# The mixer's output projection in two groups of 1024 columns, with seven block products in four of its units

## The chip, the cores and the metric

One core of one Trainium2 chip runs the kernel as a single program. The time is device microseconds of one execution; the median of three runs stands for a kernel. Engines have names of two kinds here: TensorE is PE in the profile, VectorE is DVE, ScalarE is ACT, GpSimd is POOL and SyncE is SP.

## The reference, cut to what matters

The model is two blocks on 256 tokens of width 2048, in float32. The change lies in the first block, where the token mixer ends and its norm and the cross attention begin:

```python
    merged = jax.nn.sigmoid(m_a) * (y_a @ w_proj_a) + jax.nn.sigmoid(m_b) * (y_b @ w_proj_b)
    return merged @ w_out                       # [256, 2048] @ [2048, 2048]
...
    x = x + rmsnorm(y, post_norm_mix[l])        # y is what the mixer returned
    h = rmsnorm(x, pre_norm_xa[l])
    m = rmsnorm(mem, mem_norm_g[l])
    y = memory_cross_attention(h, m, xa_wq[l], xa_wk[l], xa_wv[l], xa_wo[l])
```

rmsnorm divides a token's row by the root of the mean of its squares and multiplies it by a gain per column.

## The kernel before, in words

**Precision.** Every operand x is kept as a high part (fp32r, a rounded copy) and a low part (x minus the high part). A product is three matmuls: high by high, low operand by high weight, high operand by low weight. Weights are split while the kernel runs. SyncE loads a unit of weights (1 MiB) into one of three buffers `raw`. ScalarE copies it into `wh` (`split_hi`), VectorE writes raw minus wh into `wl` (`split_lo`), and a raw buffer is loaded again once its low part is made.

**Groups and units.** All large products are groups in one list (`groups_of`), in the order in which they run. A group is a range of output columns and is cut into units along the contraction. The kinds are: "feat" (256 columns, result turned, units of 8 k-blocks of 128), "tok" (512 columns, tokens on partitions, units of 4 k-blocks) and "wide" (1024 columns, units of 2 k-blocks). Units of the last two kinds have 24 matmuls of 512 columns. Results lie in four PSUM banks: two sets of two (`ps`). A feat or tok group uses one set, and the groups alternate. A wide group uses all four: token half 0 in the set of the group before, token half 1 in its own. Its first unit starts with token half 1 and waits for the other two banks before token half 0. Its last unit ends with token half 1. Four more banks (`pm`) serve small work.

**The stretch of the change.** The groups run mb0 to mb7 (gate), pb0 to pb7 (w_proj_b; the evacuation `evac_pb` makes the merged operand mg, 256 features a group), wo0 to wo3 (w_out, tok), xk0, xk1 (keys of the cross attention), xq0, xq1 and so on. wo's evacuation: ScalarE squares each 512-column bank for the norm's sums, then VectorE multiplies the bank by the norm's gain (`gb`) into yA. `norm1a` and `norm1b` make x1 and its scaled copy in yA, TensorE turns yA in `h2_a` (before xk1's last unit) and `h2_b` (before xq0), and both other engines split what was turned.

**Seven products.** The FFN's down projection (dw00, dw01, dw10) is wide, and in four units of each (`SEVEN`) it makes a two-by-two block product from seven products instead of eight: 21 matmuls. It needs four combinations of the operand's blocks (the forms, made once and split) and four differences of the weight's blocks (`dif_lo` and `dif_hi`, per unit: VectorE three instructions, ScalarE two, VectorE two). Some of the products gather in `pm` banks; `dw_sums` adds these into the output tile, and `evac_dw` adds the ps banks to it.

**Order of the work.** Each engine has its own strict program, written by a loop over the units. `BESIDE` maps (group, slot) to small stages that run beside a unit. For unit n, VectorE runs in this order: the stages of slot n, the differences of unit n+1 if that has seven products, token half 0 of a wide group's evacuation if n is its last unit, the low part of unit n+2, the stages of the half slot, and only then the evacuation of the group if n was its last. ScalarE runs: the high differences, the high part of unit n+2, the stages, the evacuation. Three stages of the memory's norm lie here: `mem_scale` (roots, at pb6), `mem_spread` (a small product on TensorE) and `mem_split` in four parts (sixteen instructions on each of ScalarE and VectorE). POOL loads `mem_in` (2 MiB) when mem_scale is done, `gb` after pb7, and the token rows `xx` after the last mem_split.

Of the kernel before, what the change touches and what calls it, by code (L numbers as in the profile page):

```python
# [5 lines left out]
F = mybir.dt.float32  # L6
R = mybir.dt.float32r
# [105 lines left out]
def groups_of(I):  # L113
# [28 lines left out]
    for i in range(4):  # L142
        add("wo%d" % i, I["w_out"][0], KC, [(512 * i, 512)], "tok", "mg")
# [7 lines left out]
    for half in range(2):  # L151
# [7 lines left out]
        for i in range(2 - half):  # L159
            add("dw%d%d" % (half, i), down, HF, [(1024 * i, 1024)], "wide", "ac", chunk=2, k_off=half * HF)  # L160
# [19 lines left out]
def units_of(groups):  # L180
# [63 lines left out]
    "dw00_sums": 4, "dw01_sums": 4, "dw10_sums": 4,  # L244
# [27 lines left out]
SEVEN = (2, 4, 6, 8)  # L272

# [4 lines left out]
def build(nc, I, cst_d, out_d):  # L278
# [13 lines left out]
    def by_part(both):  # L292
# [87 lines left out]
    junk_wo = tile("junk_wo", B + 4, [128, 512])  # L380
# [23 lines left out]
    dif, dif_l = [[[tile("%s%d%d" % (name, half, q), (XT if half else B) + 4 * q, [128, 1024], dt) for q in range(2)]  # L404
                   for half in range(2)] for name, dt in (("dif", F), ("dif_l", R))]
    dif_h = [[tile("dif_h%d%d" % (half, q), kb, [128, 1024], R) for q, kb in enumerate(at)]
             for half, at in enumerate(((C + 16, M + 12), (XT + 8, XT + 12)))]
# [41 lines left out]
    bst = tile("bst", B, [128, 2, 48])  # L449

# [131 lines left out]

    seven = [u.n for u in units if u.g.kind == "wide" and u.ui in SEVEN]

# [135 lines left out]
    def tensor_program(p):  # L720
# [421 lines left out]

        def wide(u):

            h, l = parts(u.n)
            p.wait_ge(*hi_ready(u.n))
            half = int(u.g.k_off > 0)
            p.wait_ge(*ready("ac", u.k + 1, half, 0))
            if u.last:
                wide_products(u, (0,), h, (ach, acl), "")  # L1150
                p.wait_ge(*lo_ready(u.n))
                wide_products(u, (0,), l, (ach,), "last").then_inc(s_acc, 1)
                wide_products(u, (1,), h, (ach, acl), "").then_inc(s_high, 1)
                wide_products(u, (1,), l, (ach,), "last").then_inc(s_used, 1)
                return
            if u.ui == 0:
                for tb in (1, 0):
# [4 lines left out]
                    t = wide_products(u, (tb,), h, (ach, acl), "")  # L1162
            else:
                t = wide_products(u, (0, 1), h, (ach, acl), "")
            t.then_inc(s_high, 1)
            p.wait_ge(*lo_ready(u.n))
            wide_products(u, (0, 1), l, (ach,), "").then_inc(s_used, 1)

        def seven_products(u):

            h, l = parts(u.n)
            half, m, j = int(u.g.k_off > 0), seven.index(u.n), 4 * SEVEN.index(u.ui)
            k, new, end = u.k, u.ui == SEVEN[0], u.ui == SEVEN[-1]
# [4 lines left out]
            a11, a12, a22 = [[x_[:, kk, t_] for x_ in (ach, acl)] for kk, t_ in ((k, lo_t), (k + 1, lo_t), (k + 1, hi_t))]  # L1178
            s1, s2, s3, s4 = [[f[:, j + i, :] for f in (form_h, form_l)] for i in range(4)]
            q11, q21, q22 = slice(0, 512), slice(1024, 1536), slice(1536, 2048)  # L1180
            p.wait_ge(*hi_ready(u.n))
            p.wait_ge(*ready("ac", k + 1, half, 0))
# [10 lines left out]
            for q, pairs in enumerate((((p5, s1, sums[1]), (p7, s3, sums[2])), ((p6, s2, sums[3]), (b21, a22, None)))):  # L1193
                d, dh = dif_l[half][q], dif_h[half][q]
# [98 lines left out]
    def scalar_program(a):  # L1293
# [37 lines left out]
        def dif_hi(n):  # L1331

            half, m = int(units[n].g.k_off > 0), seven.index(n)
            if m:
                a.wait_ge(s_diffree, m)
            for q in range(2):
                a.wait_ge(s_dif, 2 * m + q + 1)
                act(dif_h[half][q], dif[half][q], ACT.Copy).then_inc(s_difh, 1)

        def dw_sums(name):  # L1340
# [3 lines left out]
            if name == "dw10":  # L1344
# [149 lines left out]
        def evac_wo(i, blocks):  # L1494
            name = "wo%d" % i
            for tb in blocks:
                filled(name, tb)
                j = tb * 4 + i
                square("junk_wo", junk_wo, ps[set_of[name]][tb], cell("part1", 8)[:, j:j + 1])

        def norm1a():
            root("p1", 2)
            a.wait_ge(s_a2v, last["junk_wo"])
# [10 lines left out]
        def h2(part, k0):  # L1514
            a.wait_ge(s_used, after("wo3"))
# [240 lines left out]
        def evac_w2(i, blocks):  # L1756
# [11 lines left out]
            "gla_turn4": lambda: gla_turn(4), "gla_turn8": lambda: gla_turn(8), "gla_turn12": lambda: gla_turn(12),  # L1768
            "mem_sums": mem_sums, "mem_scale": mem_scale, "mem_split0": lambda: mem_split(0),
# [19 lines left out]
        def evac(name, blocks):  # L1789
# [17 lines left out]
            elif kind == "wo":  # L1807
                evac_wo(i, blocks)
# [70 lines left out]
    def vector_program(v):  # L1879
# [69 lines left out]
        def dif_lo(n):  # L1949

            half, m, r = int(units[n].g.k_off > 0), seven.index(n), v3(raw[n % 3], 512)
            d = [v3(dif[half][q], 512) for q in range(2)]
            v.wait_ge(s_ac, 11 * half + 11)
# [8 lines left out]
            for q in range(2):  # L1962
                v.wait_ge(s_difh, 2 * m + q + 1)
                lo_part(dif_l[half][q], dif[half][q], dif_h[half][q]).then_inc(s_difl, 1)
# [276 lines left out]
        def evac_pb(i):  # L2241
# [14 lines left out]
            lo_part(xtl[:, c, :], v3(m_, 256), xth[:, c, :]).then_inc(s_mg, 1)  # L2256

# [25 lines left out]
        def evac_wo(i, blocks):  # L2283
            name = "wo%d" % i
            c = slice(512 * i, 512 * i + 512)
            v.wait_ge(s_gb1, 16)
            v.wait_ge(s_used, after("pb7"))
            for tb in blocks:
                filled(name, tb)
                heard()  # L2290
                tt(yA[:, tb, c], ps[set_of[name]][tb], gb[:, c], ALU.mult).then_inc(s_accfree[set_of[name]], 1)

        def norm1a():
            v.wait_ge(*evacuated("wo2"))
            v.wait_ge(*evacuated("wo3"))
            ssq = cell("ssq1", 2)
            t = own.add(v.tensor_reduce(ssq, v3(cell("part1", 8), 4), AX.X, ALU.add))
# [20 lines left out]
        def h2(part, k0):  # L2318
            v.wait_ge(s_used, after("wo3"))
# [198 lines left out]
        def dw_sums(name):  # L2518
# [504 lines left out]
        def layer_norm(tb, scaled):  # L3023
# [37 lines left out]
            "gla_turn4": lambda: gla_turn(4), "gla_turn8": lambda: gla_turn(8), "gla_turn12": lambda: gla_turn(12),  # L3061
            "mem_sums": mem_sums, "mem_scale": mem_scale, "mem_spread": mem_spread, "mem_split0": lambda: mem_split(0),
# [28 lines left out]

        def evac(name, blocks):
            kind, i = name[:-1], int(name[-1]) if name[-1].isdigit() else 0
            if kind == "u":
# [22 lines left out]
            elif kind == "wo":  # L3117
# [235 lines left out]
```

## Time and profile before

| what | value |
|---|---|
| median of 3 runs | 2054.79 us (2054.45 to 2055.03) |
| span of the profiled execution, first to last instruction | 2053.1 us |
| TensorE busy | 2044.2 us |
| VectorE busy | 1524.8 us |
| ScalarE busy | 988.5 us |
| mean granted clock of TensorE | 1.000 |
| weights and data read | 392.09 MB, 193 GB/s over the span |

The span is what the trace shows of the profiled execution; the device time of the runs lies 1.7 us above it at the median. Busy time is the time in which an engine has an instruction in work. An idle time in a timeline stands behind the instruction that follows it, with the engine and tile that ended it. Tiles that share a place in memory share names in the profile: a unit's tiles are raw, wh and wl, the merged operand and the turned ones are xt.

### The profile page before, as it was taken

Reading aid. Unit: us, or ns where it says so; the run is one execution under the profiler, and the core shown is the slowest. Engines: PE = TensorE matmul, PEld = TensorE weight load, DVE = VectorE, ACT = ScalarE, POOL = GpSimd, SP = SyncE. Lnnn points to the kernel's source line nnn. Section 1 sums busy time; section 2 is a strip of 40 time slices with the busy share of each in tenths; the row PEclk is TensorE's granted clock in tenths of the full one; section 3 lists DMA queues with packets and bytes.
Section 4 is the critical chain, followed back from the end, with each engine's and each line's share of the span. In section 5 each row is a group of like instructions: output and inputs, shape, how many; then the busy total and the mean of one; then the engine's idle time right before and its main releaser. Section 6 shows DMA issues by size and latency. Waiting matters only on the chain.

```text
span 2053.1 us, 26543 instructions
## 1 busy us (share of the span) xinstructions
PE 2044.2 (100%) x10788; PEld 1757.5 (86%) x10788; DVE 1524.8 (74%) x1857; ACT 988.5 (48%) x986; POOL 16.0 (1%) x34
## 2 busy tenths in 40 slices
PE   9999999999999999999999999999999999999999
PEld 7888888888888888888888888888888888888987
DVE  5776786554656767678988887888886768987776
ACT  6443363454444455555554544445454434454642
POOL 0000000000000000000000000000000000000000
PEclk9999999999999999999999999999999999999999
DMA  9766656546566765555656565555566654554462
GB/s 328 220 191 194 193 167 213 180 153 210 152 198 226 259 233 185 184 186 174 209 191 200 189 202 188 194 189 192 198 212 236 185 174 144 186 184 144 144 244 105
DMA packets 298346, 397.99 MB, mean 194 GB/s; under 512 B 18945, under 2 KB 223793, under 8 KB 296561
## 3 DMA queue, kind: packets, MB, share of 16 engines
q1 hardware_dynamic: 294096, 375.28, 56.1%
q0 software_dynamic: 3408, 18.92, 2.5%
q10 hardware_dynamic: 720, 2.11, 0.3%
q8 instruction: 85, 1.39, 0.3%
q14 instruction: 37, 0.30, 0.0%
HBM read 392.09 MB, written 4.19 MB: 193 GB/s over the span
## 4 chain that ended last, share of the span: by engine, by line
PE 97%; DVE 1%; DMA 1%; ACT 1%; issue 0%; SPq 0%; DVEq 0%; ACTq 0%
PE ps L723 91%; PE pm L723 5%; PE pm L726 1%; DVE wl L1884 0%; DMA raw<-in_w_in 0%; DMA xin<-in_x_by_features 0%; DVE cv L1892 0%; ACT wh L1298 0%; ACT xt L1298 0%; DVE yA L1884 0%; DVE up L2066 0%; ACT cv L1298 0%; DVE up L1884 0%; ACT L1298 0%; DVE xt L1892 0%
## 5 line engine op out<-in xcount | busy, mean ns | idle before, releaser
L1884 DVE TENSOR_TENSOR wl<-raw,wh 128x2048 fp32r<-128x2048 f32 (+2 forms) x368 | 790.0, 2161 | 284.0 <-ACT wh L1298 211.6
L1298 ACT ACTIVATE wh<-raw 128x2048 fp32r<-128x2048 f32 (+1 forms) x357 | 664.1, 1873 | 318.6 <-PE ps L723 268.4
L723 PE MATMUL ps<-xt,wh 128*128 128x512 f32 (+2 forms) x2736 | 638.4, 389 | 0.2 <-ACT wh L1298 0.2
L723 PEld LDWEIGHTS ps<-xt,wh 128*128 128x128 f32 (+1 forms) x2736 | 505.0, 188 | 101.7 <-issue 0.7
L723 PE MATMUL ps<-wh,xt 128*128 128x512 f32 x1600 | 387.1, 391 | 1.8 <-ACT wh L1298 1.8
L723 PEld LDWEIGHTS ps<-wh,xt 128*128 128x128 f32 x1600 | 298.1, 188 | 64.5 <-issue 1.6
L723 PEld LDWEIGHTS ps<-xt,wl 128*128 128x128 f32 x2704 | 336.3, 192 | 7.0
L723 PE MATMUL ps<-xt,wl 128*128 128x256 f32 x2704 | 338.6, 283 | 0.0
L723 PE MATMUL ps<-wl,xt 128*128 128x512 f32 x800 | 203.0, 390 | 0.4 <-DVE wl L1884 0.4
L723 PEld LDWEIGHTS ps<-wl,xt 128*128 128x128 f32 x800 | 149.9, 188 | 32.7 <-DVE wl L1884 1.7
L1298 ACT ACTIVATE cv<-up,vt 128x256 f32<-128x256 f32 x88 | 52.5, 601 | 220.3 <-DVE up L1884 220.3
L723 PE MATMUL ps<-wh,ach 128*128 128x512 f32 x268 | 104.6, 390 | 0.4 <-DVE yA L1884 0.4
L723 PE MATMUL ps<-wh,acl 128*128 128x512 f32 x268 | 104.3, 389 | 0.0
L1892 DVE SCALAR_TENSOR_TENSOR cv<-up,vt,cv 128x255 f32<-128x255 f32 (+1 forms) x176 | 81.0, 481 | 6.6 <-ACT cv L1298 3.5
L723 PE MATMUL ps<-wl,ach 128*128 128x512 f32 x268 | 69.2, 389 | 0.0
L723 PEld LDWEIGHTS ps<-wh,ach 128*128 128x128 f32 x268 | 50.3, 188 | 11.8 <-DVE yA L1884 0.8
L723 PE MATMUL ps<-ybT,wh 128*128 128x512 f32 x256 | 59.9, 390 | 0.0
L723 PEld LDWEIGHTS ps<-wl,ach 128*128 128x128 f32 x268 | 50.3, 188 | 10.5
L723 PEld LDWEIGHTS ps<-wh,acl 128*128 128x128 f32 x268 | 50.3, 188 | 10.3
L2066 DVE TENSOR_REDUCE up<-ps 128x256 f32<-128x512 f32 x84 | 57.2, 684 | 0.0
L723 PEld LDWEIGHTS ps<-ybT,wh 128*128 128x128 f32 x256 | 47.4, 188 | 9.4
L1298 ACT ACTIVATE dif_h<-dif 128x1024 fp32r<-128x1024 f32 x24 | 25.5, 1063 | 50.4 <-DVE dif L1884 50.4
(405 smaller groups left out, 1601.5 us busy)
## 6 DMA issues: line engine op xcount, KB each, us to landing
raw<-in_w_in SPq DMA_DIRECT2D x146, 1024.0 KB, 5.3
raw<-in_ffn_w_up SPq DMA_DIRECT2D x84, 1024.0 KB, 5.2
raw<-in_ffn_w_down SPq DMA_DIRECT2D x43, 1024.0 KB, 5.1
raw<-in_w_out SPq DMA_DIRECT2D x32, 1024.0 KB, 5.3
raw<-in_w_proj_b SPq DMA_DIRECT2D x16, 1024.0 KB, 5.4
raw<-in_w_proj_a SPq DMA_DIRECT2D x8, 1024.0 KB, 5.4
raw<-in_xa_wk SPq DMA_DIRECT2D x4, 1024.0 KB, 5.4
raw<-in_xa_wq SPq DMA_DIRECT2D x4, 1024.0 KB, 5.3
```

The source lines that it names most:

```text
L723: return p.matmul(out, l, r, start=start, stop=stop, skip_group_check=share)
L726: return p.transpose(out, a, ident)
L1298: return a.activation(out, in_, func, bias=bias, scale=scale)
L1884: return v.tensor_tensor(out, a, b, op)
L1892: return v.scalar_tensor_tensor(out=out, in0=a, scalar=s, in1=b, op0=op0, op1=op1)
L2066: v.tensor_reduce(out, halves, AX.X, ALU.add).then_inc(s_accfree[set_of[name]], 1)
```

## The change

wo becomes two wide groups of eight units. Units 2 and 5 of each have seven products. The forms of the merged operand are made in the evacuations of pb2 and pb5 and lie in SBUF below the former lowest tile, in room that the software DMA queue's scratch gives up (16 KB to 4 KB). The stages at wo move to new slots. The evacuation now adds banks and sums into yA, ScalarE squares yA from SBUF (two instructions of 1024 columns a group), and VectorE multiplies by the gain in an instruction of its own behind that (`s_gain`). The wait on the operand in wide units stays only in the first group that uses it.

```diff
+SCRATCH = 4096
+LOW = (SCRATCH + 128 - BASE) // KB
...
-    for i in range(4):
-        add("wo%d" % i, I["w_out"][0], KC, [(512 * i, 512)], "tok", "mg")
+    for i in range(2):
+        add("wo%d" % i, I["w_out"][0], KC, [(1024 * i, 1024)], "wide", "mg", chunk=2, seven=PAIRS["mg"])
...
-    ("pb4", 0): ["mem_sums"], ("pb6", 0): ["mem_scale"], ("wo0", 2): ["mem_spread"],
-    ("wo1", 0): ["mem_split0"], ("wo1", 1): ["mem_split4"], ("wo1", 2): ["mem_split8"], ("wo1", 3): ["mem_split12"],
+    ("pb4", 0): ["mem_sums"], ("pb6", 0): ["mem_scale"], ("wo0", 0): ["mem_spread"],
+    ("wo0", 2.5): ["mem_split0"], ("wo0", 3): ["mem_split4"], ("wo0", 5.5): ["mem_split8"], ("wo0", 6): ["wo0_sums", "mem_split12"],
+    ("wo1", 6): ["wo1_sums"],
...
+PAIRS = {"mg": (2, 5), "ac": SEVEN}
...
 # ScalarE, evac_pb
             to_v.add(act(xth[:, 2 * i:2 * i + 2, :], v3(mt[i % 2], 256), ACT.Copy))
+            if i in PAIRS["mg"]:
+                j = PAIRS["mg"].index(i)
+                heard()
+                to_v.add(act(mg_form_h[:, 4 * j:4 * j + 4, :], v3(mg_form[j], 128), ACT.Copy))
...
 # ScalarE, evac_wo
-                filled(name, tb)
-                j = tb * 4 + i
-                square("junk_wo", junk_wo, ps[set_of[name]][tb], cell("part1", 8)[:, j:j + 1])
+                for n in range(2):
+                    a.wait_ge(*evacuated("wo%d" % i, 2 * tb + n))
+                j = tb * 2 + i
+                square("junk_m", junk_m, yA[:, tb, 1024 * i:1024 * i + 1024], cell("part1", 4)[:, j:j + 1])
...
 # VectorE, evac_pb: behind the low part of xt, if i in PAIRS["mg"]
+            tt(s1, a21, a22, ALU.add)
+            step(own.add(tt(s3, a21, a11, ALU.subtract)))
+            step(own.add(tt(s2, s3, a22, ALU.add)))
+            to_act.add(tt(s4, a12, s2, ALU.subtract))
+            heard()
+            lo_part(mg_form_l[:, 4 * j:4 * j + 4, :], v3(mg_form[j], 128), mg_form_h[:, 4 * j:4 * j + 4, :]).then_inc(
+                s_form["mg"], 1)
...
 # VectorE, evac_wo
-                heard()
-                tt(yA[:, tb, c], ps[set_of[name]][tb], gb[:, c], ALU.mult).then_inc(s_accfree[set_of[name]], 1)
+            i = int(name[2])
+            step(last[name])
+            filled(name, tb)
+            for n in range(2):
+                o = yA[:, tb, 1024 * i + 512 * n:1024 * i + 512 * n + 512]
+                tt(o, bank(name, 2 * tb + n), o, ALU.add).then_inc(evacuated(name, 2 * tb + n)[0], 1)
+            if tb:
+                c = slice(1024 * i, 1024 * i + 1024)
+                v.wait_ge(s_gb1, 16)
+                for b in range(2):
+                    heard()
+                    tt(yA[:, b, c], yA[:, b, c], gb[:, c], ALU.mult).then_inc(s_gain, 1)
...
 # VectorE, norm1a
-            v.wait_ge(*evacuated("wo2"))
-            v.wait_ge(*evacuated("wo3"))
+            v.wait_ge(s_gain, 4)
```

## Rows read from the trace of the kernel before

**Rows 1.** The page, part 1: busy us, share of span, instructions.
```profile
PE 2044.2 (100%) x10788; PEld 1757.5 (86%) x10788; DVE 1524.8 (74%) x1857; ACT 988.5 (48%) x986; POOL 16.0 (1%) x34
```

**Rows 2.** Windows: busy us (x count) by engine, granted clock, DMA share, GB/s.
```profile
680.00:830.00 150.00, 150.00 (x764) 128.27 (x763) 104.04 (x113) 78.70 (x93) 4.19 (x8) 1.00 0.69 238
```

**Rows 3.** TensorE timeline in wo2: start, duration us, what [idle before <-releaser].
```profile
742.42 3.79 PE L723 MATMUL ps<-wh,xt 128*128 128x512 f32 x16
...
747.86 3.79 PE L723 MATMUL ps<-wh,xt 128*128 128x512 f32 x16
```

**Rows 4.** Timeline, VectorE: the FFN's equivalent of the forms.
```profile
966.50 0.49 DVE L1884 TENSOR_TENSOR up<-cv 128x128 f32<-128x128 f32 x2
...
968.87 0.69 DVE L1884 TENSOR_TENSOR form_l<-up,form_h 128x512 fp32r<-128x512 f32 x1 [1.22 <-ACT form_h L1298]
```

**Rows 5.** Timeline of ScalarE, pb2 to pb7.
```profile
646.85 3.71 ACT L1298 ACTIVATE wh<-raw 128x2048 fp32r<-128x2048 f32 x2
...
683.71 1.28 ACT L1298 ACT_TABLE_LOAD   x1
...
686.12 1.90 ACT L1298 ACTIVATE wh<-raw 128x2048 fp32r<-128x2048 f32 x1
...
697.82 1.92 ACT L1298 ACTIVATE wh<-raw 128x2048 fp32r<-128x2048 f32 x1 [1.42 <-DMA raw<-in_w_out]
```

**Rows 6.** Timeline of VectorE, pb3 to pb7.
```profile
652.31 2.29 DVE L1884 TENSOR_TENSOR wl<-raw,wh 128x2048 fp32r<-128x2048 f32 x1 [1.23 <-PE ps L723]
...
678.35 1.28 DVE L2066 TENSOR_REDUCE mt<-ps 128x256 f32<-128x512 f32 x2
...
686.65 4.49 DVE L1884 TENSOR_TENSOR wl<-raw,wh 128x2048 fp32r<-128x2048 f32 x2
...
701.98 1.28 DVE L2066 TENSOR_REDUCE mt<-ps 128x256 f32<-128x512 f32 x2
...
705.55 0.69 DVE L1884 TENSOR_TENSOR xt<-mt,xt 128x512 fp32r<-128x512 f32 x1 [0.70 <-ACT xt L1298]
```

**Rows 7.** Timeline of TensorE: pb7 begins, wo0 begins.
```profile
687.30 7.44 PE L723 MATMUL ps<-ybT,wh 128*128 128x512 f32 x32
...
698.41 3.82 PE L723 MATMUL ps<-wh,xt 128*128 128x512 f32 x16
```

**Rows 8.** Timeline of VectorE in wo1: the low parts of memT.
```profile
727.64 1.67 DVE L1892 SCALAR_TENSOR_TENSOR memT<-mem_in,vt,memT 128x256 fp32r<-128x256 f32 x4
```

**Rows 9.** VectorE timeline where dw00 ends and dw01 begins.
```profile
1194.17 1.28 DVE L1884 TENSOR_TENSOR yA<-ps,yA 128x512 f32<-128x512 f32 x2
...
1195.37 1.82 DVE L1884 TENSOR_TENSOR wl<-raw,wh 128x512 fp32r<-128x512 f32 x2
...
1197.10 1.22 DVE L1884 TENSOR_TENSOR dif<-raw 128x1024 f32<-128x1024 f32 x1
```

**Rows 10.** Timeline of TensorE at the same place.
```profile
1195.60 0.47 PE L723 MATMUL ps<-wh,ach 128*128 128x512 f32 x1 [0.41 <-DVE yA L1884]
```

**Rows 11.** Timeline of VectorE behind the projection.
```profile
787.73 0.17 DVE L2297 TENSOR_REDUCE st<-st 128x2 f32<-128x8 f32 x1
...
799.35 1.29 DVE L1888 TENSOR_SCALAR yA<-xx,st 128x2048 f32<-128x2048 f32 x1
...
806.88 3.22 DVE L1892 SCALAR_TENSOR_TENSOR xt<-pm,vt,xt 128x256 fp32r<-128x256 f32 x8
```

**Rows 12.** TensorE timeline: xk0 begins, then the turns of yA.
```profile
785.94 3.79 PE L723 MATMUL ps<-memT,wh 128*128 128x512 f32 x16
...
802.63 1.91 PE L726 MATMUL pm<-cst,yA 128*128 128x128 f32 x16
...
809.97 1.91 PE L726 MATMUL pm<-cst,yA 128*128 128x128 f32 x16
```

**Rows 13.** By tile junk_m: count, ns min/median/max, first and last start.
```profile
L1318 ACT ACTIVATE junk_m<-xx x4: 1042/1058/1063, 659.8 to 663.4; 128x1024 f32<-128x1024 f32 x4
```

**Rows 14.** Timeline of TensorE at the start of the kernel.
```profile
1.05 5.13 PE L723 MATMUL pm<-ones 128*128 128x128 f32 x24 [1.05 <-DVE ones L3168]
```

More of the change, by code:

```diff
@@ L403, in build @@
     form_l = tile("form_l", C + 8, [128, 4 * len(SEVEN), 128], R)
[L404 to L407, printed above, removed]
+    at_dif = {"wo0": ((G + 8, G + 12), (B, B + 4)), "dw00": ((B, B + 4), (C + 16, M + 12)), "dw10": ((XT, XT + 4), (XT + 8, XT + 12))}
+    dif, dif_l = [{g: [tile("%s_%s%d" % (name, g, q), kb, [128, 1024], dt) for q, kb in enumerate(at[0])]
+                   for g, at in at_dif.items()} for name, dt in (("dif", F), ("dif_l", R))]
+    dif_h = {g: [tile("dif_h_%s%d" % (g, q), kb, [128, 1024], R) for q, kb in enumerate(at[1])] for g, at in at_dif.items()}
+    for its in (dif, dif_l, dif_h):
+        its["dw01"], its["wo1"] = its["dw00"], its["wo0"]
     part = [tile("part%d" % q, XT + 16 + 2 * q, [128, 512]) for q in range(2)]
@@ L449, in build @@
     bst = tile("bst", B, [128, 2, 48])
+    forms = {"mg": (mg_form_h, mg_form_l), "ac": (form_h, form_l)}
     def pair(x, k):
@@ L581, in bank @@
         return ps[s][n]
-    seven = [u.n for u in units if u.g.kind == "wide" and u.ui in SEVEN]
+    seven = [u.n for u in units if u.ui in u.g.seven]
     def is_seven(n):
@@ L1177, in seven_products @@
             lo_t, hi_t = slice(0, 128), slice(128, 256)
-            a11, a12, a22 = [[x_[:, kk, t_] for x_ in (ach, acl)] for kk, t_ in ((k, lo_t), (k + 1, lo_t), (k + 1, hi_t))]
-            s1, s2, s3, s4 = [[f[:, j + i, :] for f in (form_h, form_l)] for i in range(4)]
+            a11, a12, a22 = [[x_[:, kk, t_] for x_ in (xh, xl)] for kk, t_ in ((k, lo_t), (k + 1, lo_t), (k + 1, hi_t))]
+            s1, s2, s3, s4 = [[f[:, j + i, :] for f in forms[u.g.x]] for i in range(4)]
             q11, q21, q22 = slice(0, 512), slice(1024, 1536), slice(1536, 2048)
             p.wait_ge(*hi_ready(u.n))
-            p.wait_ge(*ready("ac", k + 1, half, 0))
+            if u.g.x in s_form:
+                p.wait_ge(s_form[u.g.x], len(PAIRS[u.g.x]))
+            elif first_use[u.g.name]:
+                p.wait_ge(*ready(u.g.x, k + 1, half, 0))
             for o, x_, q, first in ((p1, a11, q11, new), (b11, a12, q21, False), (b12, s4, q22, False)):
@@ L1331, in dif_hi @@
         def dif_hi(n):
-            half, m = int(units[n].g.k_off > 0), seven.index(n)
+            m, g = seven.index(n), units[n].g.name
             if m:
@@ L1514, in h2 @@
         def h2(part, k0):
-            a.wait_ge(s_used, after("wo3"))
+            a.wait_ge(s_used, after("wo1"))
             split_turned(use["h2_" + part], gcols(28), k0, xth)
@@ L1949, in dif_lo @@
         def dif_lo(n):
-            half, m, r = int(units[n].g.k_off > 0), seven.index(n), v3(raw[n % 3], 512)
-            d = [v3(dif[half][q], 512) for q in range(2)]
-            v.wait_ge(s_ac, 11 * half + 11)
+            g, m, r = units[n].g, seven.index(n), v3(raw[n % 3], 512)
+            d = [v3(dif[g.name][q], 512) for q in range(2)]
+            if g.x == "mg":
+                v.wait_ge(s_used, after("pb7"))
+            elif g.x == "ac":
+                v.wait_ge(s_ac, 11 * int(g.k_off > 0) + 11)
             if m:
@@ L2318, in h2 @@
         def h2(part, k0):
-            v.wait_ge(s_used, after("wo3"))
+            v.wait_ge(s_used, after("wo1"))
             split_turned(use["h2_" + part], gcols(28), k0, xth, xtl)
```

107 lines of the change are left out of this document (60 added, 47 removed).

## The prediction

> **What bounds the kernel now.** I read the page's busy times first: TensorE is busy for 2044.2 us of the 2053.1 us span [rows 1]. The windows come next: from 680 to 830 us, where the change works, TensorE is busy for 150.00 of 150.00 us at a granted clock of 1.00, while VectorE is busy 104 and ScalarE 79 [rows 2]. So a removed matmul is worth its slot, and any new wait is paid in full. The slot comes from the projection itself: a 24-matmul unit starts at 742.42 and the next at 747.86, so 5.44 us / 24 = 0.227 us [rows 3]. What the reader is to see in the other rows is how late VectorE runs here. It is a strict queue, and it serves the evacuation of a group only behind the low part of the unit after next.
>
> **What is removed.** Four units issue 21 matmuls instead of 24: 4 x 3 x 0.227 = 2.7 us less. Everything below asks what it costs.
>
> **The forms, made in the evacuations of pb2 and pb5.** The FFN's equivalent begins at 966.50 and its last instruction (form_l) ends at 969.56, with two ScalarE copies in between; here there is one (0.62 us), so 1.15 us to the end of the fourth form, 0.1 + 0.62 + 0.05 for ScalarE, 0.7 for the low part: 2.6 us in VectorE's queue [rows 4]. ScalarE is held too, since its copy stands ahead of the next weight split.
> - pb2: ScalarE's copy of its result ends as the two splits begin (646.85, 3.71 us) [rows 5], and VectorE's low part of it, 0.7 us, follows, to about 647.7. With the form copy at 648.9 to 649.5 the two splits end at 651.4 and 653.2. VectorE's low part that began at 652.31, bound by TensorE [rows 6], now queues behind the previous one: 651.45 + 2.25 = 653.7. So 1.4 us late. From there to pb5 the queue never waits for TensorE again (the tags name ScalarE) [rows 6], so the lateness stays: pb5's evacuation moves from 678.35 to 679.7.
> - pb5: plus 2.6, so all behind it is 3.9 to 4.0 us late. ScalarE's split for pb7's first unit, which ended where the table load begins (683.71), then ends at 687.6, and that for the second (686.12 to 688.0) at 691.9. TensorE wants them at 687.3 and 3.6 us later [rows 5, 7]: 0.4 + 0.7 = 1.1 us of stall.
> - mem_in's four loads are issued 3.9 us later, and with them the tile of wo0's second unit, which landed at 697.82, 8.9 us after its issue at 688.9 (the end of the first of the two low parts of 686.65) [rows 5, 6]. I take 701.7.
>
> **The start of wo0.** A 1024-column group needs all four banks. Before, wo0 needed only pb6's two. The program does token half 1 first (8 matmuls, 1.8 us), then waits for both of pb7's banks. pb7's reductions ran at 701.98 to 703.26, behind the low part of the tile that landed at 697.82 [rows 5, 6], while TensorE had left pb7 at 698.4 [rows 7]. Even with no lateness: 698.35 + 0.6 (mem_spread, now in front) + 1.8 = 700.8, wait to 703.4, 2.6 us. With 3.9 us of lateness pb7's banks are read at 707.15; TensorE's unstalled arrival is 700.8, so by then it has lost 6.5 us (1.1 in pb7, 0.3 for wo0's first high part, 5.1 here). Bounds for this step: 1.5 (tile landed early, no lateness) and 7.5. I take 6.5.
>
> By the Trainium skill ("DMA: Bandwidth & Descriptors", the two cost components) a transfer costs a fixed 2 us plus its bytes at a fixed rate, an estimate of 4.4 us for this 1 MiB tile. By that rule the late tile would not hold VectorE, and the sum would be about 1.4 us lower; the trace has 8.9 us here behind mem_in's 2 MB.
>
> **Through wo0 to wo1.** VectorE's queue from pb7's first reduction to wo0's last add, from rows: pb7's evacuation 4.3 (701.98 to 706.24) [rows 6]; mrb's copy of 256 columns 0.4, taken as a memT; six full low parts at 2.25 (two in 4.49) = 13.5 [rows 6]; two short ones at 1.8 = 3.6; two sets of differences, each three of 1024 columns at 1.2 and two of 512 at 0.7, 10.1 [rows 9]; sixteen memT at 0.42 = 6.7 [rows 8]; four sums at 0.69, 2.75; four bank adds 2.6 [rows 9]; three waits of 0.7 for ScalarE's split behind the differences, 2.1. Sum 46.1 us. TensorE from the same point to where wo1's first unit wants wo0's last banks: 1.4 + (16 + 24 + 21 + 24 + 24 + 21 + 24 + 24 + 8) x 0.227 = 43.6. VectorE ends last, by 2.6 us with its semaphore. The same place in the FFN, where no memT work lies beside, cost 0.4 us (TensorE at 1195.60) [rows 10]. Bounds 0.4 and 3.5; I take 2.6. A clock shift at the start doesn't change it, since both run from the same event. The norm weights' products in wo1 (2 x 1.2) are hidden: VectorE has gaps of several us in that group, as before.
>
> **The norm behind wo1.** T is the end of the projection on TensorE, 785.9 before [rows 12]. Before: last evacuation (ScalarE's squares, then VectorE), reduction at 787.73 = T+1.8, the second scaled half ends 800.64 = T+14.7, and TensorE turns it at 802.63 = T+16.7 [rows 11, 12]. So there are 1.9 us of slack. Now: token half 0 is added at T-2.5, the low part runs to T+1.0, the last two adds end T+2.3; ScalarE's square over 1024 takes 1.24 (T+3.65) [rows 13]; VectorE's two weight products 1.2 each, the second behind that square, end T+4.95; reduction T+5.1, against T+1.8, so 3.3 us later. The rest is the same chain: root behind ScalarE's split, four x1 parts, squares, a split, two roots. Scaled half at T+18.0, turned at T+18.2: 1.5 us of stall. Bounds 0 (all in the slack) and 2.1.
> Then h2_b: each of its banks waits for VectorE's h2_a, which ran 806.88 to 810.1, end to end with what precedes it [rows 11], so it is 3.3 us late too (last bank free T+27.5). TensorE would turn h2_b at T+25.35 to T+27.1 and now ends at T+28.1: 1.0 us. Bounds 0 and 1.5. The products of xq0 then find their operands; VectorE catches up behind.
>
> **Other edits.** Dropped waits, the s_gain semaphore and the shorter reduction: nothing, all on free engines. The smaller scratch of the software DMA queue: its 34 issues take 16.0 us of POOL in all [rows 1], none waited for; I take 0, bounds 0 and 1. wo's tiles come in longer rows, as ffn_w_down's do: 0, since no tile ends a wait beyond the one named.
>
> **Sum.** -2.7 + 6.5 + 2.6 + 1.5 + 1.0 = +8.9 us. The profiled span is 2053.1; the runs' median of 2054.8 lies 1.7 us above it, which is outside the first and last instruction and stays. 2054.8 + 8.9 = 2063.7 us.
>
> **Rivals.**
> - The lateness of the forms is made up before pb7 (one free us per group is enough to undo most). Then only 2.6 at the start: -2.7 + 2.6 + 2.6 + 1.5 + 1.0 = +5.0, 2059.8 us. For it: pb's groups last 11.1 us and VectorE's own work in them about 9. Against: mem_scale's roots sit right behind pb5.
> - Not slower: the transitions cost what the one in the FFN does, 0.4 us each [rows 10], and the norm stays in its slack. -2.7 + 0.8 = -1.9, 2052.9 us. It would need VectorE to reach pb7's and wo0's banks within 1.8 us of TensorE. It decides at the order of the queue: only if the low part ahead of the evacuation is ready early. For it stands 1195.60 [rows 10], against it 701.98 [rows 6]. Even free of all stalls the time is 2052.1.
> - TensorE's clock. The granted clock is 1.00 here, with no gap before it [rows 2]. The kernel's first 24 matmuls of 128 columns, out of rest, took 5.13 us, 0.21 each; later ones of that size 1.91 us for sixteen, 0.12 [rows 12, 14]. If the new 5.1 us gap has the same effect for as long, it costs 5.1 / 2 = 2.6 us, hidden in the 2.6 us that VectorE is behind anyway; after the second gap it would not be: 2066.3 us.
>  The Trainium skill ("TensorE: Matmul & The Clock Gate", the clock gate and the practical rules) says that TensorE falls back to its lower level when left idle between bursts; no row here shows a fall.
>
> **How the numbers follow.** Forecast 0.50 (2061.5 to 2066), forms made up 0.24, clock or a further wait 0.12, not slower 0.14. 0.2% is 4.1 us, about what can be told from no change: the bounds are 2050.7 and 2058.9. Slower takes the forecast, the clock case and four fifths of the second: 0.82. Same 0.16, faster 0.02. The range is 2057.0 to 2067.5: it leaves out the not-slower case and little else.
>
> **What would show it.** TensorE's waits: some 5 us in wo0's first unit, released by VectorE's mt reductions; 2 to 3 us in wo1's first, by yA; 1 to 2 before the first turn of yA, 1 on its second. Seven-product units of 4.76 us. pb5's evacuation near 679.7 and mem_in's issue near 691. Wrong, if the chain of waits shows TensorE alone through 700 to 830.

## The result, and the profile after

The changed kernel takes **2063.32 us** (median of 5 runs, 2062.41 to 2063.80) and the kernel before, beside it, 2054.61 us (2054.30 to 2055.03). The ratio is 1.004, 95% interval 1.003 to 1.0051: slower by 8.7 us. The forecast was 2063.7 us. The profiled execution took 2062.63 us with a span of 2060.8 us, 7.7 us above before's span. The medians below leave out two executions that lie far from the others of their kernel: one of the kernel before, timed beside e5 to e8 (4782.52 us), and one of e8 (2529.18 us at a mean granted clock of 0.752).

Windows first: the stretch and its length, busy us of TensorE, its weight loads, VectorE, ScalarE and GpSimd, then the granted clock, the DMA share and GB/s, as in [rows 2]:

```profile
680.00:830.00 150.00, 143.10 (x709) 120.24 (x708) 128.09 (x152) 83.70 (x95) 4.19 (x8) 0.99 0.64 223
705.00:708.00 3.00, 0.68 (x2) 0.62 (x3) 2.87 (x4) 0.00 (x0) 0.00 (x0) 0.81 0.98 401
708.00:709.00 1.00, 1.00 (x4) 0.82 (x3) 0.69 (x1) 0.20 (x1) 0.00 (x0) 0.50 0.71 279
708.00:712.00 4.00, 4.00 (x14) 3.20 (x13) 2.40 (x5) 2.43 (x2) 0.00 (x0) 0.71 0.75 295
712.00:716.00 4.00, 4.00 (x19) 3.33 (x18) 3.90 (x6) 1.29 (x2) 0.00 (x0) 1.00 0.00 0
```

TensorE, which was busy for all of the 150 us, is now idle for 6.9 of them; VectorE works 24 us more. The rows from 705 to 712 us show something that the stretch did not have before: the granted clock falls, to 0.50 from 708 to 709 us, the lower of its two levels (1.2 GHz), and is back at 1.00 (2.4 GHz) from 712 us on. The 0.81 and 0.71 are means over both levels. Where TensorE stands, its timeline tells (start, duration, what, idle time and releaser), to be laid beside [rows 7, 12]:

```profile
691.49 3.92 PE L735 MATMUL ps<-ybT,wh 128*128 128x512 f32 x16 [0.39 <-ACT wh L1315]
...
699.08 0.61 PE L735 MATMUL pm<-dg,ones 128*128 128x128 f32 x4
699.86 2.11 PE L735 MATMUL ps<-wh,xt 128*128 128x512 f32 x8 [0.17 <-ACT wh L1315]
707.32 3.45 PE L735 MATMUL ps<-wh,xt 128*128 128x512 f32 x8 [5.35 <-DVE mt L2092]
...
717.90 0.62 PE L735 MATMUL pm<-wh,xt 128*128 128x512 f32 x2
...
722.66 1.52 PE L735 MATMUL ps<-wh,xt 128*128 128x512 f32 x6
...
749.18 1.98 PE L735 MATMUL ps<-wh,xt 128*128 128x512 f32 x8
751.57 2.06 PE L735 MATMUL ps<-wh,xt 128*128 128x512 f32 x8 [0.41 <-DVE yA L1907]
...
809.28 1.86 PE L738 MATMUL pm<-cst,yA 128*128 128x128 f32 x15 [0.32 <-DVE yA L1911]
...
816.58 2.83 PE L738 MATMUL pm<-cst,yA 128*128 128x128 f32 x16
```

And VectorE's queue, against [rows 6]: the form, then pb7's evacuation behind the low part of a tile that it waits for, a low part in wo0, and the first pair of bank adds at wo0's end.

```profile
685.33 0.69 DVE L1907 TENSOR_TENSOR mg_form_l<-mg_form,mg_form_h 128x512 fp32r<-128x512 f32 x1 [0.70 <-ACT mg_form_h L1315]
...
703.69 2.29 DVE L1907 TENSOR_TENSOR wl<-raw,wh 128x2048 fp32r<-128x2048 f32 x1 [1.55 <-ACT wh L1315]
705.89 1.28 DVE L2092 TENSOR_REDUCE mt<-ps 128x256 f32<-128x512 f32 x2
...
711.32 1.83 DVE L1907 TENSOR_TENSOR wl<-raw,wh 128x512 fp32r<-128x512 f32 x2 [0.83 <-DVE mrb L2313]
...
746.74 1.29 DVE L1907 TENSOR_TENSOR yA<-ps,yA 128x512 f32<-128x512 f32 x2 [0.50 <-PE ps L735]
```

Added up against before (a slot is the time from one group of matmuls to the next without a wait): pb7 ends at 699.08 instead of 698.41 (+0.7); wo0's first matmuls come 0.78 behind the four small ones, where 0.36 is their pace in the kernels below that don't wait (+0.4); the eight of them need 1.81, so the gap to 707.32 is 5.65 (+5.65). The next eight fill 3.29 us up to 710.61, where 1.81 is their slot (+1.5, the clock). At 749.18 eight matmuls again, and 2.39 us to the next (+0.6). Four seven-product units of 4.76 us (717.90 to 722.66) give back 2.7. xk0 begins at 792.00, against 785.94: +6.1. The turns of yA lose 0.6 and, with 2.83 us for sixteen against 1.91 [rows 12], 0.9. Together +7.6, of 7.7 in the span.

### The profile page after: what moved, and what is told of

The parts are those of the page before. It is cut to its first block, busy times and chain, and to the rows that moved or that the text cites. A ratio compares the mean times of both kernels' runs of the same rounds, so it can differ in the third digit from the quotient of the medians.

```text
span 2060.8 us, 26580 instructions
## 1 busy us (share of the span) xinstructions
PE 2045.2 (99%) x10776; PEld 1757.4 (85%) x10776; DVE 1554.9 (75%) x1903; ACT 997.8 (48%) x990; POOL 16.0 (1%) x34
## 4 chain that ended last, share of the span: by engine, by line
PE 92%; DVE 3%; ACT 2%; DMA 1%; issue 1%; SPq 0%; DVEq 0%; ACTq 0%
PE ps L735 86%; PE pm L735 5%; PE pm L738 1%; DVE wl L1907 1%; ACT wh L1315 1%; DMA raw<-in_w_out 0%; DMA raw<-in_w_in 0%; ACT xt L1315 0%; DVE yA L1907 0%; DMA xin<-in_x_by_features 0%; DMA raw<-in_xa_wq 0%; DVE cv L1915 0%; DVE mt L2092 0%; DVE xt L1915 0%; DVE mt L1907 0%
## 5 line engine op out<-in xcount | busy, mean ns | idle before, releaser
L735 PE MATMUL ps<-wh,xt 128*128 128x512 f32 x1544 | 376.1, 392 | 7.3 <-DVE mt L2092 5.3
L735 PEld LDWEIGHTS ps<-wh,xt 128*128 128x128 f32 x1544 | 289.0, 189 | 69.0 <-DVE mt L2092 5.7
L735 PE MATMUL ps<-wl,xt 128*128 128x512 f32 x772 | 196.5, 390 | 0.4 <-DVE wl L1907 0.4
L735 PEld LDWEIGHTS ps<-wl,xt 128*128 128x128 f32 x772 | 144.7, 188 | 31.6 <-DVE wl L1907 1.7
L1315 ACT ACTIVATE dif_h_dw<-dif_dw 128x1024 fp32r<-128x1024 f32 x24 | 25.5, 1062 | 50.4 <-DVE dif_dw L1907 50.4
```

Source lines behind the costliest of these rows:

```text
L735: return p.matmul(out, l, r, start=start, stop=stop, skip_group_check=share)
L1315: return a.activation(out, in_, func, bias=bias, scale=scale)
```

## The experiments

Each was timed beside the kernel before: its median was 2054.87 us for e1 to e4, 2054.79 for e5 to e8, 2054.89 for e9 to e11. The theory V is the prediction's: VectorE's strict queue sets every new wait. The first four kernels ask how the price divides.

**e1: the wide groups without forms and seven-product units.** The copies stand for adds into sums.

```
-PAIRS = {"mg": (2, 5), "ac": SEVEN}
+PAIRS = {"mg": (), "ac": SEVEN}
...
-                tt(o, bank(name, 2 * tb + n), o, ALU.add).then_inc(evacuated(name, 2 * tb + n)[0], 1)
+                v.tensor_copy(o, bank(name, 2 * tb + n)).then_inc(evacuated(name, 2 * tb + n)[0], 1)
```

> The changed kernel without its seven-product units: two 1024-column groups, all sixteen units with 24 matmuls, no forms, no differences, no sums; the evacuation copies the banks into yA. Theory V (the loss comes from VectorE's queue: the forms make it late, a 1024-column group must wait for pb7's banks, the differences keep VectorE behind to the end of wo0, the norm's chain is longer): the 2.7 us of matmuls come back, pb7 has no wait, the wait in wo0's first unit falls from 5.3 to some 2.6 us, no loss between wo0 and wo1 over 0.5, the turns behind stay as they are (1.5 us). 2054.6 + 2.6 + 0.4 + 1.5 = 2059.1 us. Rival (the seven-product units and their VectorE work are the whole loss, the wide grouping costs nothing): 2054.6 us.

2061.28 us (2060.12 to 2063.25), ratio 1.0031 [1.0018, 1.0043]. Its TensorE:

```profile
698.28 0.61 PE L734 MATMUL pm<-dg,ones 128*128 128x128 f32 x4
698.64 2.09 PE L734 MATMUL ps<-wh,xt 128*128 128x512 f32 x8
703.82 2.85 PE L734 MATMUL ps<-wh,xt 128*128 128x512 f32 x8 [3.08 <-DVE mt L2091]
...
749.63 2.06 PE L734 MATMUL ps<-wh,xt 128*128 128x512 f32 x8 [0.41 <-DVE yA L2330]
```

And VectorE at wo0's end:

```profile
744.79 1.29 DVE L2330 COPY yA<-ps 128x512 f32<-128x512 f32 x2 [3.69 <-PE ps L734]
```

The wait at wo0's start is there without any form. The wide groups alone lose 6.4 us; the change loses 8.7 and has 2.7 fewer in matmuls, so its costs are 11.4 us, and a little over half of them belong to the 1024-column groups, whose first unit wants four banks. V missed by 2.2 us: from 703.82 to xk0 at 791.42 are 87.6 us for 376 matmuls, which are worth 376 x 0.2267 = 85.2. Of the rest, 0.6 goes at wo1's start (2.39 us for eight matmuls instead of 1.81) and about 1.7 is the clock, which I had left out. Here VectorE isn't behind: it waits 3.69 us for TensorE at wo0's end, so nothing hides the fall. TensorE loses 0.6 at wo1's start even so, because a low part stands between VectorE's two pairs of bank reads.

**e2: the kernel before, with the forms made and not used.** Four adds, ScalarE's copy and the low part, as in the change, at pb2 and pb5; the scratch of the software DMA queue is the smaller one too.

```
+            if i in MG:
...
+                tt(s1, a21, a22, ALU.add)
+                step(own.add(tt(s3, a21, a11, ALU.subtract)))
+                step(own.add(tt(s2, s3, a22, ALU.add)))
+                to_act.add(tt(s4, a12, s2, ALU.subtract))
+                heard()
+                own.add(lo_part(mg_form_l[:, 4 * j:4 * j + 4, :], v3(mg_form[j], 128), mg_form_h[:, 4 * j:4 * j + 4, :]))
```

> The kernel before, with the forms made in the evacuations of pb2 and pb5 (and with the smaller scratch of the software DMA queue), and nobody reading them. Theory V: VectorE and ScalarE are 3.5 us later from pb5 on, but the 512-column groups wait for no bank of pb7, so only pb7's late weight split is paid: +0.8 us, 2055.4 us. Rival (the lateness is itself the loss and reaches TensorE wherever it goes): +3.5 us, 2058.1 us. If the smaller scratch costs anything it is in this run too, above 0.8 us.

2056.64 us (2056.25 to 2057.09), ratio 1.0008 [0.9999, 1.0017], 1.8 us above before:

```profile
691.58 3.96 PE L729 MATMUL ps<-ybT,wh 128*128 128x512 f32 x16 [0.40 <-ACT wh L1304]
...
699.95 3.92 PE L729 MATMUL ps<-wh,xt 128*128 128x512 f32 x16 [0.58 <-ACT wh L1304]
```

wo0 begins 1.54 us later than in [rows 7], at two waits for ScalarE's splits: the lateness does reach pb7, as predicted, and "made up before pb7" falls. V had 0.8 us, so it missed by 1.0: it counted the wait in pb7 and not the one at wo0's first tile. These waits are nearly all of the 1.7 us by which the span is longer than before's, so nothing visible is left for the smaller scratch.

**e3: VectorE reads pb7's banks before the low part of wo0's second unit.** Nothing else is moved.

```
+            early = u.g.name == "pb7" and u.last
+            if early:
+                leave(u)
             if u.n + 2 < NU and not moved_low(u.n + 2):
                 split_lo(u.n + 2)
...
-            leave(u)
+            if not early:
+                leave(u)
```

> The changed kernel, with VectorE reading pb7's banks ahead of the low part of wo0's second unit instead of behind it. Theory V: the reductions start at about 702.1 instead of 705.9, the wait in wo0's first unit falls from 5.3 to 1.8 us and TensorE keeps its clock, but VectorE's queue stays full to the end of wo0 and gains only the 1.6 us for which it waited on that tile; the rest comes back as a wait of some 4 us in wo1's first unit. 2063.3 - 1.6 = 2061.7 us. Rival (each wait stands for itself): 3.8 us of wait and 1.5 us of slow matmuls go, 2058.0 us.

2059.68 us (2059.55 to 2060.22), ratio 1.0024 [1.0015, 1.0033]: 3.6 us better than the change's median, and 2.9 us between the two profiled spans (2057.9 and 2060.8). V gave 1.6, the rival 5.3.

```profile
703.65 2.08 PE L735 MATMUL ps<-wh,xt 128*128 128x512 f32 x8 [1.50 <-DVE mt L2092]
...
745.31 2.06 PE L735 MATMUL ps<-wh,xt 128*128 128x512 f32 x8 [1.03 <-DVE yA L1907]
748.70 2.06 PE L735 MATMUL ps<-wh,xt 128*128 128x512 f32 x8 [1.34 <-DVE yA L1907]
```

The gap shrinks from 5.35 to 1.50, the clock stays at 1.00, and part of the gain comes back at wo0's end as 1.03 and 1.34. That is V's signature: VectorE worked from 702.22 to 748.56 with three waits of 0.5 to 0.7 us for ScalarE, and its end is the bound. It ended 2.9 us sooner than in the change, because three waits of its own had gone: 1.55 us for the late tile, 0.83 ahead of the next low part (711.32) and 0.50 for TensorE at 746.74. V had counted only the first.

**e4: 22 idle matmuls in the gap.** They write a spare bank and keep TensorE at work; their sums are not used.

```
+                    if tb == 0 and u.g.name == "wo0":
...
+                        for _ in range(FILL):
+                            mm(fb, xh[:, 0, 0:128], h[:, 0:512], True, True)
```

> The changed kernel, with 22 idle matmuls of 512 columns into a spare bank in the gap of wo0's first unit (their result is read by nobody). Theory V: the granted clock stays at 1.00, the 1.5 us of slow matmuls behind the gap go, and come back as a longer wait in wo1's first unit (0.6 to 2.1 us), since VectorE ends last there: 2063.3 us, within 0.4. Rival (the clock's fall is part of the sum): 2061.8 us. In both the spread of the runs should shrink if it comes from the clock.

2062.12 us (2061.82 to 2062.61), ratio 1.0035 [1.0022, 1.0047]; the span is 2060.8, that of the change.

```profile
702.23 5.16 PE L736 MATMUL pm<-wh,xt 128*128 128x512 f32 x22
707.85 2.08 PE L736 MATMUL ps<-wh,xt 128*128 128x512 f32 x8 [0.46 <-DVE mt L2098]
...
751.51 2.09 PE L736 MATMUL ps<-wh,xt 128*128 128x512 f32 x8 [1.22 <-DVE yA L1913]
```

The eight matmuls at 707.85 take 1.92 us up to the next, not 3.29. But these matmuls at wo1's start come at 751.51, in the change at 751.57: 0.8 us came back as a longer wait for VectorE (1.22 instead of 0.41). The fall was not hidden whole. The profiled execution of e4 was already 0.4 us behind that of the change at pb0, at 609 us, and from there to xk0 it takes 182.3 us against 182.7; in the change VectorE waits 0.50 us for TensorE at 746.74, in e4 it doesn't. So about 0.4 of the 1.5 us are paid and the rest is hidden. The median is 1.2 us below that of the change, which was timed in another set of runs, and nearer to the rival's 2061.8 than to V's 2063.3. The two executions of the change whose mean clock was 0.998 took 2063.63 and 2063.80 us, the three at 0.999 2062.41 to 2063.32; it fits that a longer fall gets past the cover, but no profile of such an execution of the change shows it.

The next four take the waits away one after another.

**e5: e3, and mem_in's splits in wo1.**

```
-    ("wo0", 2.5): ["mem_split0"], ("wo0", 3): ["mem_split4"], ("wo0", 5.5): ["mem_split8"], ("wo0", 6): ["wo0_sums", "mem_split12"],
+    ("wo0", 6): ["wo0_sums"],
+    ("wo1", 0.5): ["mem_split0"], ("wo1", 2.5): ["mem_split4"], ("wo1", 3): ["mem_split8"], ("wo1", 3.5): ["mem_split12"],
```

> e3's kernel, and mem_in's four splits (16 VectorE instructions of 0.42 us, 6.7 us) moved out of wo0 into wo1, where VectorE had gaps in the changed kernel. Theory V (VectorE's queue from pb7's banks to wo0's last add is the bound: in e3 it ran without a gap from 702.22 to 748.56, and TensorE stood 1.03 + 1.34 us at wo0's last unit and wo1's first, plus small slots): these waits fall to about 0.4 us in all, the start of wo0 (1.5 us), the 0.8 to 1.0 us in pb7 and the turns' 1.4 us stay. About 2057.2 us, 2.5 below e3's 2059.7. Rival (wo1 can't take the work): VectorE, now the later of the two at the end of wo1, reaches the norm later by what it gained: waits move to the first turn of yA, about 2059.5 us.

2060.86 us (2060.67 to 2061.28), ratio 1.0029 [1.0018, 1.0041], 1.2 us above e3: the waits of wo0's end went, as V said (only 0.41 at 746.79), and came back at xk0 (1.60) and at the first turn (1.52), as the rival said. Why is seen in e6.

**e6: e5, the forms' split deferred, the low part first.** VectorE's four adds stay in pb2 and pb5; ScalarE's copy and the low part of the forms go to wo0's second unit.

```
+    ("pb4", 0): ["mem_sums"], ("pb6", 0): ["mem_scale"], ("wo0", 0): ["mem_spread"], ("wo0", 0.5): ["mg_split"],
...
+            late = u.g.kind == "wide" and u.last and u.g.name[:2] == "wo"
+            if u.g.kind == "wide" and u.last and not late:
                 evac_wide(u.g.name, 0)
...
                 split_lo(u.n + 2)
+            if late:
+                evac_wide(u.g.name, 0)
```

> e5's kernel, and two edits more. One: the four adds of each form stay in the evacuations of pb2 and pb5, but ScalarE's copy of the forms and VectorE's low part of them run at wo0's second unit, ahead of the first seven-product unit. Two: in wo0's and wo1's last unit VectorE computes the low part of the unit after next ahead of token half 0's adds. Theory V: the waits of pb7 (0.8 to 1.0 us) and most of wo0's start (1.5 us to about 0.5) go, the turns' waits fall from 1.5 to about 0.3 us; what is left is -2.7 + 0.5 + 0.4 + 0.3 us against before: about 2053.3 us. Rival (the waits have another cause, mem_in's 2 MiB ahead of wo0's second tile, and the norm's chain as such): no gain over e5, about 2057 us.

2058.71 us (2057.96 to 2059.36), ratio 1.0018 [1.001, 1.0027]. Both theories missed. From pb7 to wo1's end TensorE waits for nothing; then it loses at one place all that had been gained. TensorE, ScalarE and VectorE there:

```profile
782.13 1.07 PE L736 MATMUL ps<-wl,xt 128*128 128x512 f32 x4
786.98 5.67 PE L736 MATMUL ps<-memT,wh 128*128 128x512 f32 x16 [3.79 <-issue]
```

```profile
776.48 1.92 ACT L1316 ACTIVATE wh<-raw 128x2048 fp32r<-128x2048 f32 x1 [3.78 <-DMA raw<-in_xa_wk]
```

```profile
781.78 4.49 DVE L1911 TENSOR_TENSOR wl<-raw,wh 128x2048 fp32r<-128x2048 f32 x2
786.20 2.48 DVE L1911 TENSOR_TENSOR yA<-ps,yA 128x512 f32<-128x512 f32 x4
```

xk0 starts at 786.98, just behind the first of VectorE's four adds of 786.20, which read the banks; the row names no releaser ("issue"), so the bank is inferred. These adds wait behind two low parts, those behind the group's sums, those behind ScalarE's, and ScalarE's stands behind the split of xa_wk's first tile, which waited 3.78 us for its data. The DMA issues (durations in ns, first and last start in us) show what stood ahead of that tile:

```profile
L3330 POOL DMA_DIRECT2D xx<-in_x x2: 527/527/527, 765.7 to 766.2; - x2
L3278 SPq DMA_DIRECT2D raw<-in_xa_wk x4: 367/368/368, 768.1 to 784.1; - x4
```

x's 2 MiB go into mem_in's memory, so they start behind its last split: in the change at 744.3, here at 765.7, 2.4 us ahead of the tile, which landed 8.4 us after its issue. And after this gap too the clock falls, to 0.50 from 788 to 790 us: sixteen matmuls take 5.67 us instead of 3.79.

**e7: the change, with e6's second edit alone.**

> The changed kernel with edit two alone: in wo0's and wo1's last unit VectorE computes the low part of the unit after next ahead of token half 0's adds. Theory V (as predicted, the low part stands between the two pairs of adds and the norm's products follow the last add): the norm's first scaled half comes some 1 us sooner or not at all, depending on whether the low part was waiting for TensorE; the turns' stalls (0.6 + 0.9 us) go in part, at wo0's end little moves. 2061.9 us, bounds 2061.2 and 2063.3. Rival (the turns' stalls come from ScalarE's squares of yA, not VectorE's order): 2063.3 us, as the changed kernel.

2062.40 us (2061.97 to 2063.52), ratio 1.0037 [1.0024, 1.0051]. From xk0 to the first scores the kernel before takes 53.55 us, the change 55.04, this one 54.34: the last two adds start at T+0.27 (T is xk0's start) instead of T+0.96, and the 0.7 us arrive in full. The first turn's stall is gone, and 0.8 of the second's is left. The span is that of the change all the same, 2060.8: the gap at wo0's start is longer here (5.73), the fall of the clock behind it costs 2.4 us, and at wo0's end VectorE waits 0.72 us for TensorE, so nothing hides it.

**e8: the change, with the norm's weights on 32 of 1024 columns.** Most of that product is left out.

```
-                    tt(yA[:, b, c], yA[:, b, c], gb[:, c], ALU.mult).then_inc(s_gain, 1)
+                    part_c = slice(1024 * i, 1024 * i + 32)
+                    tt(yA[:, b, part_c], yA[:, b, part_c], gb[:, part_c], ALU.mult).then_inc(s_gain, 1)
```

> The changed kernel with the norm's weights multiplied on 32 of each 1024 columns only (most of that product is left out): VectorE's two products behind each group take about 0.1 us instead of 1.29 each. Theory V: the second group's 2 x 1.2 us stood between wo1's last add and the norm's reduction, so the reduction moves from T+4.65 to about T+2.9 (ScalarE's square of token half 1 then ends last), and the turns' 1.5 us of stall nearly go: 2062.0 us. Rival (ScalarE's squares over 1024 columns set the reduction anyway, since the second of them ends with the products): 2063.3 us.

2063.08 us (four executions, 2062.67 to 2063.59), ratio 1.004 [1.0026, 1.0054]: near the rival's 2063.3; V is wrong here. ScalarE, then VectorE:

```profile
794.30 1.06 ACT L1335 ACTIVATE junk_m<-yA 128x1024 f32<-128x1024 f32 x1 [2.24 <-DVE yA L1907]
...
795.36 1.90 ACT L1315 ACTIVATE wh<-raw 128x2048 fp32r<-128x2048 f32 x1
797.16 0.18 ACT L1315 ACTIVATE st<-st 128x2 f32<-128x2 f32 x1
```

```profile
795.59 0.15 DVE L2342 TENSOR_REDUCE st<-st 128x2 f32<-128x4 f32 x1
...
797.38 0.17 DVE L1945 RECIPROCAL st<-st 128x2 f32<-128x2 f32 x1 [1.43 <-ACT st L1315]
```

The reduction came 1.06 us sooner, and then waited 1.43 us for ScalarE, whose root stands behind a weight split, which stands behind the square of token half 1. The reciprocal is at 797.38; in the change it is at 797.40. The products were covered by ScalarE's queue.

The last three test the reading of e6.

**e9: e6, with x's loads out of the tile's way.**

```
+    ("wo0", 6): ["wo0_sums"],
+    ("wo0", 5.5): ["mem_split0"],
+    ("wo1", 0.5): ["mem_split4"], ("wo1", 2.5): ["mem_split8"], ("wo1", 3): ["mem_split12"],
...
-        e.wait_ge(s_memx, 16)
         for tb in range(2):
+            e.wait_ge(s_memx, 8 * tb + 8)
             e.dma_start(xx[:, tb, :], x_src[:, tb, :]).then_inc(s_x2nd, 16)
```

> e6's kernel with mem_in's splits one place earlier (one at wo0's sixth unit, three in wo1) and x's two loads each started as its half of mem_in is read, not both behind the last split. Theory X (e6 had no wait of TensorE from pb7 to the end of wo1, 2.75 us ahead of the kernel before; it lost 3.79 us and a clock fall at xk0, because x's 2 MiB, issued at 765.7, stood ahead of xa_wk's first tile, issued at 768.1 and landed 8.4 us later, and two low parts then stood ahead of the adds that free xk0's bank): with x's loads gone from there the wait and the fall go. TensorE stays 2.75 us ahead up to xk0 and loses 0.8 us at the second turn: about 2052.9 us. Rival (the bank's adds come late whatever the tile does, since the low parts stand ahead of them): some 2 to 4 us of wait stay at xk0, 2055 to 2058 us.

**2052.95 us** (2052.60 to 2053.99), ratio 0.9991 [0.9982, 0.9999]: 1.9 us below before (inside the 0.2% that the prediction counts as no change, though the interval ends below 1) and 10.4 us below the change.

```profile
L3331 POOL DMA_DIRECT2D xx<-in_x x2: 530/530/530, 749.7 to 762.9; - x2
L3279 SPq DMA_DIRECT2D raw<-in_xa_wk x4: 367/368/368, 767.0 to 779.9; - x4
```

```profile
698.69 0.61 PE L737 MATMUL pm<-dg,ones 128*128 128x128 f32 x4
699.05 3.92 PE L737 MATMUL ps<-wh,xt 128*128 128x512 f32 x16
...
783.51 3.79 PE L737 MATMUL ps<-memT,wh 128*128 128x512 f32 x16
...
800.21 1.91 PE L740 MATMUL pm<-cst,yA 128*128 128x128 f32 x16
...
807.54 2.70 PE L740 MATMUL pm<-cst,yA 128*128 128x128 f32 x16
```

The tile's split now waits 0.70 us and begins at 772.33. xk0 starts 2.4 us ahead of before; 0.8 us is left at the second turn.

**e10: the same two edits on e5.**

> The same two edits on e5's kernel (forms made whole in the evacuations, adds ahead of the low part). Theory X: of e5's waits the 1.60 us at xk0 goes and the 1.52 us at the first turn falls to about 0.5; 1.51 us at wo0's start, 0.4 at wo1's and pb7's stay: about 2058.2 us. Rival: VectorE has no room in wo0 for the one split moved back, 1.7 us come back as a wait at wo1's start: about 2060 us.

2057.85 us (2057.21 to 2058.49), ratio 1.0014 [1.0006, 1.0023], 3.0 us below e5. xk0 doesn't wait, the first turn waits 0.32; the 1.51 at wo0's start and 0.41 at wo1's are there as before. In e9 the low parts still stand ahead of the adds and xk0 doesn't wait, and here the gain is there with the adds in the change's order as well; ScalarE's wait for the tile's data went from 3.78 us (e6) to 0.70 (e9). So the loads were the cause, and not the rival of e9. Which of the two edits frees them, the split moved forward or the loads started by halves, was not tried apart.

**e11: e9 with units of 24 matmuls.** No forms, differences or sums.

> e9's kernel without the seven-product units: four units of 24 matmuls again, no forms, no differences, no sums. Theory: in a kernel without stalls the twelve matmuls are worth their slots, so this one is 12 x 0.227 = 2.7 us slower than e9: 2055.6 us if e9 is 2052.9. Rival: the sums and differences on VectorE and ScalarE cost e9 a part of it, and the distance is below 2 us.

2055.49 us (2055.21 to 2056.62), ratio 1.0003 [0.9994, 1.0012], 2.5 us above e9.

The TensorE of e11, and that of e9 where pb0 begins:

```profile
609.12 3.82 PE L736 MATMUL ps<-ybT,wh 128*128 128x512 f32 x16
...
698.06 0.61 PE L736 MATMUL pm<-dg,ones 128*128 128x128 f32 x4
...
785.62 3.79 PE L736 MATMUL ps<-memT,wh 128*128 128x512 f32 x16
```

```profile
609.74 3.82 PE L737 MATMUL ps<-ybT,wh 128*128 128x512 f32 x16
```

From the small matmuls to xk0 it is 87.56 us here and 84.82 in e9: 2.74 us, against 12 x 0.227 = 2.72. Between the profiled spans (2053.5 and 2051.6) it is 1.9: that execution of e9 was already 0.6 us later where pb0 begins, ahead of the first form, and from there to the small matmuls both take the same time (88.94 and 88.95 us). So the sums, the differences and the forms' adds cost e9 nothing that shows, and the rival of e11 falls.

## Why the prediction was right

- **Removed matmuls, 2.7 us:** right; 4.76 us a unit, and 2.74 between e9 and e11.
- **Start of wo0, 6.5 us:** right in size (6.7) and in mechanism. The parts are 0.7 (1.1 forecast), 0.4 (0.3) and 5.65 (5.1). e1 divides it: 3.4 us of gap without any form. With the forms VectorE reads pb7's banks 3.5 us later than in e1 (705.89 against 702.39), of which 1.2 reaches TensorE as earlier stalls (699.86 against 698.64) and 2.3 lengthens the gap.
- **VectorE 3.9 us late at pb7's banks:** 3.9 came (705.89 against 701.98), in part by luck. The forms made VectorE 3.4 us late, not 3.9 (pb6's reductions at 694.46 instead of 691.05); the tile of wo0's second unit, issued 3.4 us later, then took 9.3 us to land where 8.9 had been read, and VectorE waited for it.
- **VectorE last at wo1, 2.6 us:** too high. The row at wo1 shows 0.6 us, which e1 has too, with VectorE idle before it: it comes from the low part between the two pairs of adds. With the clock's 1.5 the two make 2.1, near the forecast by luck. Without the fall (e4) TensorE loses 1.4 us there, and this is the size of the term; that the full queue is its cause is borne out by e3, which still waits 1.03 and 1.34 us there, and e5, which is left with the 0.6 once mem_in's splits are gone from wo0.
- **The clock:** the fall did come, at 1.5 us in the profiled execution against 2.6 in the rival's working, and it was hidden but for about 0.4 us (e4). The trace agrees with the cited rule of the Trainium skill ("TensorE: Matmul & The Clock Gate", the clock gate) on falling back when idle between bursts: 0.50 from 708 to 709 us, behind a gap of 5.35. It was a rival that could be true together with the forecast.
- **The tile's landing:** the estimate from "DMA: Bandwidth & Descriptors" (the two cost components) in the Trainium skill, 4.4 us, would have had the tile early. It landed 9.3 us after its issue: VectorE waited 1.55 us at 703.69 on the split, which had waited 1.94 for the data.
- **First turn, 1.5 us:** the term that was mis-sized, 0.6 measured. The chain came 0.45 us sooner (reduction at T+4.65), and the two products that I had put on it weren't on it: e8 takes them away and nothing moves. The term's mechanism, "VectorE's two weight products", is wrong; the right one is the late adds and ScalarE's square, split and root behind them (e7, e8).
- **Second turn, 1.0 us:** 0.9. The working has the unstalled turn at T+25.35; by its own rows it is 809.97 - 785.94 + 1.5 = T+25.5, which gives 0.9.
- **Not slower, 2052.9 us:** fell, at the point that it named: VectorE reached pb7's banks 5.65 us behind TensorE. The floor that it gave, 2052.1 us free of all stalls, is 0.9 us below e9, which has 0.8 us left at the second turn.
- **The signs:** 5.35 us in wo0's first unit by the mt reductions, 0.9 on the second turn, units of 4.76 us, pb5's evacuation at 679.32 and mem_in's issue at 690.4 came as named. The 2 to 3 us in wo1's first unit (0.41) and the 1 to 2 before the first turn (0.32) did not.
- **Total:** +8.9 forecast, +7.7 in the span and +8.7 between the medians. Too high were the turn (0.9), wo1's start with the clock (0.5) and pb7 (0.4); too low was the gap (0.55). That the median lies only 0.4 us from the forecast is partly luck: it is 0.7 above the profiled execution. It fits the clock's variation, which the sum didn't have, but no profile shows it.

## What to carry to other kernels

A group that needs more accumulators at its start inherits the lateness of whoever empties them; look at where the evacuation stands in its engine's queue, and at what that queue waits for in front of it, before counting the matmuls saved. Moving work to a "free" stretch also moves every transfer that waits for its memory: here x's 2 MiB, started 21 us later in e6, stood ahead of the next group's first tile, and e5, where they were moved first, came out 1.2 us above e3. Take a product off the path only after seeing which of two engines the next step waits for.

## What was not expected of the hardware

TensorE's granted clock fell to 0.50 after gaps of 5.35 us (the change), 3.08 (e1), 3.79 (e6) and 5.73 (e7), and stayed at 1.00 after 1.50 (e3), 1.51 (e5 and e10) and 1.60 (e5, at xk0). None of the gaps in this stretch lay between 1.60 and 3.08 us. What it took differs: 1.5 us in the change, 1.7 in e1, 1.9 in e6, and in e7 sixteen matmuls needed 6.0 us instead of 3.6. It differs between executions of one kernel too, and their times follow it. Of e6's eleven, five have a mean clock of 0.999 and took 2057.96 to 2058.67 us, six have 0.998 and took 2058.71 to 2059.36. Of e1's six, three at 1.000 took 2060.12 to 2060.84, two at 0.999 2061.71 and 2062.11, and one at 0.998 2063.25.
